# The last 128 tokens' LayerNorm split over VectorE, ScalarE and GpSimd, in one layer of a pooling and mLSTM decoder

## The reference

```
def _layer_norm(x, g, b):
    xf = x.astype(jnp.float32)
    mu = jnp.mean(xf, axis=-1, keepdims=True)
    xc = xf - mu
    var = jnp.mean(xc * xc, axis=-1, keepdims=True)
    return (xc * lax.rsqrt(var + LN_EPS) * g.astype(jnp.float32) + b.astype(jnp.float32)).astype(x.dtype)
...
    x1 = _layer_norm(ALPHA * x + mix, ln1_g, ln1_b)
    ff = jnp.square(jax.nn.relu(x1 @ w_ff1 + b_ff1)) @ w_ff2 + b_ff2
    x2 = _layer_norm(ALPHA * x1 + ff, ln2_g, ln2_b)
```

## Time and profile before

| | us |
|---|---|
| median of 3 runs | 1047.95 (1047.92 to 1048.46) |
| the profiled execution | 1048.17 |
| its span, first to last instruction | 1046.6 |
| TensorE busy | 1036.3 |
| VectorE busy | 747.9 |
| ScalarE busy | 495.6 |
| GpSimd busy | 101.6 |

### The profile page before, as it was taken

How to read it: one execution, slowest core, us unless ns; L and a number is a source line. 1 busy time by engine, 2 the same in 40 slices (tenths; PEclk the granted TensorE clock), 3 DMA queues, 4 the chain that set the end, 5 groups by cost and what they waited for, 6 DMA issues and landing times. The chain is left out here.

```text
span 1046.6 us, 19119 instructions
## 1 busy us (share of the span) xinstructions
PE 1036.3 (99%) x7761; PEld 1023.6 (98%) x7761; DVE 747.9 (71%) x1034; ACT 495.6 (47%) x711; POOL 101.6 (10%) x140
## 2 busy tenths in 40 slices
PE   9999999999999999999999999999999999999997
PEld 9999999999899999999999999999999999999986
DVE  6795775535797596876766767768766677887977
ACT  6554534345533576664664564565443323334223
POOL 3112221020211000000000000000000000000027
PEclk9999999999999999999999999999999999999999
DMA  9546996165224215245455445499634415325304
GB/s 283 144 176 153 246 199 135 61 165 126 71 102 141 102 41 216 98 142 185 129 157 185 141 153 183 148 296 344 229 122 166 159 62 182 122 93 172 122 3 160
DMA packets 97780, 159.95 MB, mean 153 GB/s; under 512 B 6485, under 2 KB 52277, under 8 KB 96681
## 3 DMA queue, kind: packets, MB, share of 16 engines
q1 hardware_dynamic: 88290, 127.72, 37.9%
q0 software_dynamic: 9152, 30.79, 11.3%
q10 hardware_dynamic: 270, 0.49, 0.2%
HBM read 111.56 MB, written 53.29 MB: 158 GB/s over the span
## 5 line engine op out<-in xcount | busy, mean ns | idle before, releaser
L2623 PE MATMUL bank<-x_hi,w_hi 128*128 128x344 f32 (+1 forms) x696 | 227.5, 327 | 0.2 <-DVE x_lo L1774 0.2
L2623 PE MATMUL bank<-x_hi,d_lo 128*128 128x258 f32 x968 | 222.4, 282 | 0.0
L2623 PE MATMUL bank<-x_lo,w_hi 128*128 128x344 f32 (+1 forms) x696 | 222.0, 319 | 0.0
L2623 PE MATMUL bank<-x_hi,w_lo 128*128 128x344 f32 x528 | 168.7, 319 | 0.0
L2623 PEld LDWEIGHTS bank<-x_hi,d_lo 128*128 128x128 f32 x968 | 165.7, 189 | 0.0
L2623 PEld LDWEIGHTS bank<-x_hi,w_hi 128*128 128x128 f32 (+1 forms) x696 | 130.4, 187 | 1.0 <-DVE x_lo L1774 0.5
L2623 PEld LDWEIGHTS bank<-x_lo,w_hi 128*128 128x128 f32 (+1 forms) x696 | 130.2, 187 | 0.4
L2623 PE MATMUL bank<-x_hi,s_hi 128*128 128x258 f32 x352 | 99.5, 283 | 0.0
L2623 PE MATMUL bank<-x_lo,s_hi 128*128 128x258 f32 x352 | 99.3, 282 | 0.0
L2623 PEld LDWEIGHTS bank<-x_hi,w_lo 128*128 128x128 f32 x528 | 99.2, 188 | 0.0
L2623 PE MATMUL bank<-t_hi,s_hi 128*128 128x258 f32 x336 | 95.2, 283 | 0.0
(11 more groups left out here) (463 smaller groups left out, 2570.7 us busy)
## 6 DMA issues: line engine op xcount, KB each, us to landing
h_ops<-h_unit SPq DMA_DIRECT2D x56, 258.0 KB, 7.3
x_lo_raw<-h_ops SPq DMA_DIRECT2D x14, 1032.0 KB, 5.3
s_raw<-in_w_ff SPq DMA_DIRECT2D x14, 1024.0 KB, 6.9
x_lo_raw<-h_ops SPq DMA_DIRECT2D x14, 774.0 KB, 4.5
d_raw<-in_w_ff SPq DMA_DIRECT2D x9, 1024.0 KB, 7.9
w_raw<-in_w_in SPq DMA_DIRECT2D x16, 512.0 KB, 7.1
h_ops<-t_out SPq DMA_DIRECT2D x28, 258.0 KB, 7.6
d_raw<-in_w_ff SPq DMA_DIRECT2D x8, 768.0 KB, 6.4
```

The costliest lines, as they stand in the source:

```text
L2623: return nc.tensor.matmul(out, lhsT, rhs, start=start, stop=stop, skip_group_check=True)
```

## The change

Tile 8 alone is changed. Its columns are cut in three parts, LAST: 0 to 255, 256 to 511, 512 to 1023.

- Columns 0 to 255: ScalarE writes y * (1/std) - mean/std from the bank into OUT[2] (one Identity pass of 256 columns); GpSimd multiplies by the gain and then adds the bias in OUT[2]; SyncE's queue stores 120 rows of 1 KB.
- Columns 256 to 511 and 512 to 1023: VectorE centres and multiplies by the gain in two instructions, before and behind the reciprocal, and writes the two output parts. ScalarE's queue stores each, 120 rows of 1 KB and of 2 KB.
- VectorE has a tensor_scalar of one column more, -mean/std, which ScalarE's pass takes as bias.
- VectorE's first output part now also waits for ScalarE's pass (l2_norm), and no longer for l2_numbers.
- The sample rows' store stands behind the new store in SyncE's queue, and SyncE's last wait counts one store more.

```
-            for t in (7, 8):
-                ln2_first_half(t)
-                ln2_second_half(t)
-                ln2_centred_gain(t)
-                ln2_scale(t)
-            n = L2T[8][1]
+            ln2_first_half(7)
+            ln2_second_half(7)
+            ln2_centred_gain(7)
+            ln2_scale(7)
+            ln2_first_half(8)
+            ln2_second_half(8)
...
+            dve.wait_ge(l2_stats, 2 * 8 + 2)
+            last_centred(1)
+            ln2_scale(8)
+            dve.wait_ge(l2_numbers, N_NUMBERS)
+            V.tensor_scalar(L[:, 17:18], L[:, 12:13], L[:, 16:17], -1.0, ALU.mult, ALU.mult).then_inc(l2_numbers, 1)
+            last_centred(2)
             dve.wait_ge(l2_g, 9 - N_NORMED)
-            dve.wait_ge(l2_numbers, 2 * N_NORMED + 9 - N_NORMED)
+            dve.wait_ge(l2_norm, 2 * 8 + 1)
             dve.wait_ge(out_done[2], 32)
-            for half in range(2):
-                stt(OUT[2][0:n, 512 * half:512 * (half + 1)], bank[L2_BANK[8] + half][0:n, :], LNT[0:n, 2, 16:17],
-                    GB[0:n, 1, 512 * half:512 * (half + 1)], ALU.mult, ALU.add).then_inc(l2_last, 1)
+            last_out(1)
+            dve.wait_ge(l2_g, 10 - N_NORMED)
+            last_out(2)
```

last_centred(x) is the scalar_tensor_tensor of the centring on part x alone, last_out(x) that of the output. On ScalarE:

```
             l2_root(8)
...
+            act.wait_ge(l2_numbers, N_NUMBERS + 1)
+            act.wait_ge(out_done[2], 32)
+            A(OUT[2][0:n, 0:256], bank[L2_BANK[8]][0:n, 0:256], ACT.Identity,
+              bias=LNT[0:n, 2, 17:18], scale=LNT[0:n, 2, 16:17]).then_inc(l2_norm, 1)
+            for x in (1, 2):
+                cs = slice(*LAST[x])
+                act.wait_ge(l2_last, x)
                 act.dma_start(a["y_prompt"][0, t0:SEQ, cs], OUT[2][0:SEQ - t0, cs]).then_inc(out_done[2], 16)
```

On GpSimd and on SyncE:

```
+            n, cs = L2T[8][1], slice(*LAST[0])
+            pool.wait_ge(l2_norm, 2 * 8 + 1)
+            G.tensor_tensor(OUT[2][0:n, cs], OUT[2][0:n, cs], GB[0:n, 0, cs], ALU.mult).then_inc(l2_pool, 1)
+            pool.wait_ge(l2_pool, N_NORMED + 1)
+            G.tensor_tensor(OUT[2][0:n, cs], OUT[2][0:n, cs], GB[0:n, 1, cs], ALU.add).then_inc(l2_b, 1)
...
+            sp.wait_ge(l2_b, 9)
+            sp.dma_start(a["y_prompt"][0, t0:SEQ, cs], OUT[2][0:SEQ - t0, cs]).then_inc(out_done[2], 16)
             sp.wait_ge(l2_last, 2)
             sp.dma_start(a["y_sample"][:, 0, :], OUT[2][SEQ - L2T[8][0]:L2T[8][1], :]).then_inc(out_done[2], 16)
             for s in range(3):
-                sp.wait_ge(out_done[s], 48 + 32 * (s == 2))
+                sp.wait_ge(out_done[s], 48 + 48 * (s == 2))
```

More of the change, by code:

```diff
@@ L530, in build_layer @@
         N_NORMED = 3
+        N_NUMBERS = 2 * N_NORMED + 9 - N_NORMED
+        LAST = ((0, 256), (256, 512), (512, 1024))
         def tail_cols(b):
@@ L748, in _ @@
                 token_dma(sp, OUT[t % 3][0:L2T[t][1], :], a["y_prompt"], a["y_sample"], t, False, out_done[t % 3], L2T)
+            t0, cs = L2T[8][0], slice(*LAST[0])
+            sp.wait_ge(l2_b, 9)
+            sp.dma_start(a["y_prompt"][0, t0:SEQ, cs], OUT[2][0:SEQ - t0, cs]).then_inc(out_done[2], 16)
             sp.wait_ge(l2_last, 2)
@@ L1523, in _ @@
             l2_root(8)
-            t0 = L2T[8][0]
-            for half in range(2):
-                cs = slice(512 * half, 512 * (half + 1))
-                act.wait_ge(l2_last, half + 1)
+            t0, n = L2T[8]
+            act.wait_ge(l2_numbers, N_NUMBERS + 1)
[5 more added lines that the diff above has]
+                act.wait_ge(l2_last, x)
                 act.dma_start(a["y_prompt"][0, t0:SEQ, cs], OUT[2][0:SEQ - t0, cs]).then_inc(out_done[2], 16)
@@ L2605, in _, with last_part, last_centred, last_out @@
                 ln2_scale(t)
-            for t in (7, 8):
-                ln2_first_half(t)
-                ln2_second_half(t)
-                ln2_centred_gain(t)
-                ln2_scale(t)
-            n = L2T[8][1]
+            ln2_first_half(7)
[4 more added lines that the diff above has]
+            ln2_second_half(8)
+            n, L = L2T[8][1], LNT[0:L2T[8][1], 2, :]
+            def last_part(x):
+                c0, c1 = LAST[x]
+                return bank[L2_BANK[8] + c0 // 512][0:n, c0 % 512:c0 % 512 + c1 - c0]
+            def last_centred(x):
+                c0, c1 = LAST[x]
+                stt(last_part(x), last_part(x), L[:, 12:13], GB[0:n, 0, c0:c1], ALU.subtract, ALU.mult).then_inc(l2_g, 1)
+            def last_out(x):
+                c0, c1 = LAST[x]
+                stt(OUT[2][0:n, c0:c1], last_part(x), L[:, 16:17], GB[0:n, 1, c0:c1], ALU.mult, ALU.add).then_inc(l2_last, 1)
+            dve.wait_ge(l2_stats, 2 * 8 + 2)
[4 more added lines that the diff above has]
+            last_centred(2)
             dve.wait_ge(l2_g, 9 - N_NORMED)
-            dve.wait_ge(l2_numbers, 2 * N_NORMED + 9 - N_NORMED)
+            dve.wait_ge(l2_norm, 2 * 8 + 1)
             dve.wait_ge(out_done[2], 32)
-            for half in range(2):
-                stt(OUT[2][0:n, 512 * half:512 * (half + 1)], bank[L2_BANK[8] + half][0:n, :], LNT[0:n, 2, 16:17],
-                    GB[0:n, 1, 512 * half:512 * (half + 1)], ALU.mult, ALU.add).then_inc(l2_last, 1)
+            last_out(1)
+            dve.wait_ge(l2_g, 10 - N_NORMED)
+            last_out(2)
         @block.tensor
```

## The result

The changed kernel takes 1050.54 us (median of 14 runs, 1050.19 to 1050.82) against 1048.32 us for the kernel before (14 runs, 1047.92 to 1048.84). The ratio is 1.0021, with a 95% interval of 1.0013 to 1.0028: 2.2 us slower, where 0.3 us faster was forecast and 1048.5 was the upper end of the range. The profiled execution took 1050.43 us, with a span of 1048.8 us against 1046.6.

The account below looks back on a forecast made before the run. TensorE was taken to be busy for 1036.3 of 1046.6 us, so only the tail could move. Earlier stores were to bring the last landing 0.3 us forward: 1047.95 - 0.3 = 1047.65 us, range 1047.1 to 1048.5.

Parts of the forecast that it names:

- first part: The account of what bounds the kernel: TensorE busy nearly throughout, only the tail of the last 7 us can move.
- The close: After SyncE's release at about 1045.6: the core closes about 1.0 us later.
- the sum: The tail's step-by-step times on the profile's clock, with GpSimd's second step ending at 1042.83 and 0.3 us gained.
- sign of being wrong altogether: Whole kernel: a span moved by more than 1 us, or a shift of anything ahead of the aggregate at 1039.62.
- VectorE's gain: Last tile on VectorE: the output parts end at 1042.46 where it was 1042.72, giving back 0.26 us.
- ScalarE's pass: Last tile, 256 columns on ScalarE: 0.56 us, from 1040.70 to 1041.26, taken between 0.38 and 0.77.
- GpSimd's steps: Last tile, gain and bias of columns 0 to 255: 0.67 us each, from 1041.41 to 1042.83.
- SyncE: its store: SyncE's queue at the end: 120 KB store issued at 1042.86, sample rows' store moved from 1042.75 to about 1043.20.
- The last landing: End of the last store: about 1045.3 against 1045.6, 0.3 us earlier, with 2.1 us for the sample store.
- Rival (b): At the end: GpSimd steps of 0.75 us delay SyncE's sample store, which lands at 1046.2; 1048.55 us, chance 0.22.
- its threshold: For Rival (b): sample store issued later than 1045.6 less its landing, 1042.8 with 2.8 us, 1043.5 with 2.1.
- A chance of 0.03: Whole kernel: the chance given to slower by more than 0.2%; within 0.2% had 0.95, faster 0.02.

Follow-up runs that it names:

- the small programs: Separate programs, nothing of the layer: 512 KB loads, then GpSimd memset and tensor_tensor; DRAIN excess 0.05 us without loads, 0.14 with one, 5.79 with seventy, 0.05 with SyncE's seventy.
- first and fourth experiment: First: changed kernel without its two new GpSimd steps, 1048.54 us; fourth: the same with tile 7's output on VectorE, 1047.47 us; kernel before 1048.33 us.
- the uneven halves: Kernel before with an early GpSimd DRAIN and last tile's outputs cut at column 768, 1048.42 us; with tile 7 on VectorE too, 1048.58; kernel before 1048.63.

## Why the prediction was wrong

The step that failed is in its first part: "SyncE then stands for 2.5 us until the last of these stores has landed; it is released at about 1045.6, and the core closes about 1.0 us later", and from it the tail "VectorE until 1042.7, a store of 2.8 us, a close of 1.0 us". The close was taken for a fixed price. Of its 1.0 us, 0.2 are the hand-shake behind the last DRAIN, 0.2 SyncE's own way to its DRAIN, and 0.5 waiting for GpSimd's, which ran beside the stores until 1046.3. The row stood in the trace of the kernel before, in the view of line L70, and SyncE's waits had 0.7 us there. "GpSimd is idle from 1040.71" was read from the timeline, which doesn't list a DRAIN; the queue was 5.6 us from done.

With that, no gain on the store path was worth anything while GpSimd's DRAIN set the end, a delay of up to 0.5 us on it cost nothing, and any delay of GpSimd's last operation counted in full. The last of these is why the change is slower. By that reading the sum would have been 1042.83 + 5.6 + 0.2 = 1048.6 on the profile's clock against 1046.6: 2.0 us slower, where 2.2 were measured. The prediction's own sign of being wrong altogether, a span moved by more than 1 us, came true.

The other terms, one by one, counted from the aggregate's start, since that moved by 0.08 us:

- VectorE's gain: 0.26 forecast, 3.10 - 2.88 = 0.22 measured. The 256-column operations took 0.49 (0.48).
- ScalarE's pass: 0.56, as taken from between 0.38 and 0.77.
- GpSimd's steps: 0.72 each, not 0.67; the affine_select of 0.71 was the better row. The result was complete 3.25 us behind the aggregate, 3.21 by the sum.
- SyncE: its store came 0.03 us behind GpSimd's end, as in the sum, and the sample rows' store 0.39 later, where the sum has 0.34. Counted from the aggregate it was issued at 1043.37 - 1039.70 = 3.67, 0.09 later than forecast.
- The last landing: 0.3 us earlier was forecast, and it was the same. ScalarE's stores did land earlier, by 0.4 us (5.20 against 5.60 above). The sample rows' store, now the last, undid it: issued 0.09 us later than forecast, it took 1045.7 - 1043.37 = 2.3 us and not 2.1, and the two together are the missing 0.3. In the changed kernel with the early DRAIN it took 2.3 too (1044.21 to 1046.55).

Rival (b), slower by way of GpSimd and SyncE, had the sign and the engine but not the mechanism: it put the delay on the store that GpSimd's columns wait for, gave 1048.55, and needed three pessimistic figures. None was needed. Its path was the last of the stores all the same: with a landing of 2.3 its threshold, 1045.6 less the landing, is 1043.3, which is where the sample rows' store was issued. That the last landing then came out as before is the meeting of two paths and no sign that the change left the stores alone. A chance of 0.03 for slower by over 0.2% came from "all that is moved lies in a stretch of 6 us", which held, with a wait in it that was not in the sum.

## What to carry to other kernels

Before work is moved to an engine that "is idle at the end", read the rows of the program's close for every engine, the queue's DRAIN among them, and see which ends last; a timeline of operations doesn't show it. A GpSimd that has issued many DMAs needs time behind its last operation to close (5.6 us behind 90 DMAs here), so its last operation belongs early, or an explicit DRAIN behind its last DMA, in idle time, pays that price where it costs nothing.

## What the runs showed of the hardware

- GpSimd's closing DRAIN took 5.6 us beyond its last operation in every kernel of this layer without an early one, behind a tensor_tensor of 256 or of 1024 columns, and 5.7 behind a memset. It belongs to the DMAs that GpSimd issued itself since the last DRAIN: in the small programs 0.1 us for one and 5.7 for seventy of 512 KB, nothing for seventy by SyncE.
- An early DRAIN takes the price over (5.58 us at 991.5), and the closing one is then done within 0.1 us.
- A store of 32 KB by SyncE behind one of 120 KB took 2.3 us from issue to landing in both kernels in which it was the last one (the changed kernel, without and with the early DRAIN).
- A 512 KB store that is still under way can take back what earlier issues gain: SyncE's DRAIN came 6.3 us behind the aggregate with it and 5.95 without it (first and fourth experiment, one execution each). That is not general: at the issue times of the kernel before, moving it away changed nothing (1046.1 - 1039.92 and 1045.8 - 1039.62 are both 6.2), nor did it with the uneven halves.
